# Gate projection of two token tiles as seven Strassen block products, with its weights prepared during the first feed-forward half

## What is computed

```python
D_MODEL = 1024; SEQ = 2048; D_FF = 2816; PLE_DIM = 256
...
hn = rmsnorm(h, g_ffn_norm[i])
h = h + (jax.nn.silu(hn @ w_gate[i]) * (hn @ w_up[i])) @ w_down[i]
gate = jax.nn.sigmoid(rmsnorm(h, g_ple_norm[i]) @ w_ple_gate[i])
h = h + gate * (p[i] @ w_ple_proj[i])
```

## Time and profile before

| | |
|---|---|
| median of three runs | 2041.3 us |
| span of the profiled execution | 2043.8 us |
| TensorE busy | 2014.7 us (99%), 9565 matmuls |
| VectorE busy | 1365.8 us (67%) |
| ScalarE busy | 900.5 us (44%) |
| GpSimd busy | 409.9 us (20%) |
| granted TensorE clock, mean | 0.997 of full |
| down section of half 0, us from the span's start | about 977 to 1187 |
| gate-and-embedding sections of half 0 | 1187 to 1297.5 |
| gate-and-embedding sections of half 1 | 1928 to 2038 |

### The profile page before, as it was taken

How to read it: one execution, slowest core, us unless ns; L and a number is a source line. 1 busy time by engine, 2 the same in 40 slices (tenths; PEclk the granted TensorE clock), 3 DMA queues, 4 the chain that set the end, 5 groups by cost and what they waited for, 6 DMA issues and landing times.

```text
span 2043.8 us, 26178 instructions
## 1 busy us (share of the span) xinstructions
PE 2014.7 (99%) x9565; PEld 1667.4 (82%) x9565; DVE 1365.8 (67%) x1904; ACT 900.5 (44%) x1461; POOL 409.9 (20%) x534
## 2 busy tenths in 40 slices
PE   8999999999999999999999999999999999999998
PEld 7887877877788888888888888888888888888887
DVE  4686664767686665665888765966566566987763
ACT  4585743757433333333333553533333333334542
POOL 5554644645420000000000220000000000001220
PEclk9999999999999999999999999999999999999999
DMA  8667556563933223224815029432322328342143
GB/s 194 196 186 249 192 187 219 176 237 128 347 133 122 89 70 96 83 73 165 313 57 170 21 78 237 139 119 68 95 87 69 99 80 290 138 148 81 50 134 103
DMA packets 195488, 292.10 MB, mean 143 GB/s; under 512 B 14661, under 2 KB 116429, under 8 KB 194080
## 3 DMA queue, kind: packets, MB, share of 16 engines
q1 hardware_dynamic: 172672, 212.97, 34.3%
q0 software_dynamic: 22544, 77.46, 11.2%
q10 hardware_dynamic: 144, 0.00, 0.0%
HBM read 223.25 MB, written 67.51 MB: 142 GB/s over the span
## 4 chain that ended last, share of the span: by engine, by line
PE 86%; DVE 5%; DMA 3%; issue 2%; ACT 2%; POOL 1%; SPq 0%; ACTq 0%; DVEq 0%; POOLq 0%
PE bank L2646 13%; PE bank L2648 13%; PE bank L2650 13%; PE bank L2685 7%; PE bank L2683 7%; PE bank L2684 7%; PE bank L2345 5%; PE bank L2347 5%; PE bank L2346 5%; PE bank L2321 2%; PE bank L2323 2%; PE bank L2322 2%; PE bank L2414 1%; DMA w_parts<-w_split 1%; PE bank L2427 1%
## 5 line engine op out<-in xcount | busy, mean ns | idle before, releaser
L2646 PE MATMUL bank<-a_hi,ring_hi 128*128 128x512 f32 x1232 | 480.4, 390 | 1.1 <-DVE ring_lo L1940 0.7
L2650 PE MATMUL bank<-a_hi,ring_lo 128*128 128x512 f32 x1232 | 479.9, 390 | 0.0
L2648 PE MATMUL bank<-a_lo,ring_hi 128*128 128x512 f32 x1232 | 479.9, 390 | 0.0
L2646 PEld LDWEIGHTS bank<-a_hi,ring_hi 128*128 128x128 f32 x1232 | 231.3, 188 | 50.1 <-DVE ring_lo L1940 1.4
L2650 PEld LDWEIGHTS bank<-a_hi,ring_lo 128*128 128x128 f32 x1232 | 231.3, 188 | 48.1
L2648 PEld LDWEIGHTS bank<-a_lo,ring_hi 128*128 128x128 f32 x1232 | 231.4, 188 | 47.5
L2683 PE MATMUL bank<-d_hi 128*128 128x512 f32 x616 | 240.1, 390 | 0.0
L2684 PE MATMUL bank<-d_lo,d_hi 128*128 128x512 f32 x616 | 240.0, 390 | 0.0
L2685 PE MATMUL bank<-d_hi,d_lo 128*128 128x512 f32 x616 | 239.9, 389 | 0.0
L1419 ACT ACTIVATE d_hi<-keep 128x1024 fp32r<-128x1024 f32 x132 | 139.8, 1061 | 201.9 <-PE bank L2685 184.9
L999 POOL DMA_DIRECT2D hidden_T<-hid x88 | 47.6, 541 | 770.5 <-DVE hid L1976 751.2
(11 more groups left out here) (271 smaller groups left out, 3889.9 us busy)
## 6 DMA issues: line engine op xcount, KB each, us to landing
w_parts<-w_split POOLq DMA_DIRECT2D x88, 512.0 KB, 4.6
hidden_T<-hid POOLq DMA_DIRECT2D x88, 256.0 KB, 2.3
raws<-in_w_gate SPq DMA_DIRECT2D x80, 256.0 KB, 4.7
raws<-in_w_up SPq DMA_DIRECT2D x80, 256.0 KB, 5.2
keep<-hidden_T SPq DMA_DIRECT2D x66, 256.0 KB, 3.8
raw<-in_w_ple_gate SPq DMA_DIRECT2D x64, 256.0 KB, 4.2
keep<-in_w_down SPq DMA_DIRECT2D x44, 256.0 KB, 4.1
other<-hidden_T SPq DMA_DIRECT2D x44, 256.0 KB, 6.8
```

The costliest lines, as they stand in the source:

```text
L2646: mm(dst[:, :], wh[:, g, cols], a_hi[o][:, k, :], start=fresh and k == 0, stop=False, skip_group_check=True)
L2648: mm(dst[:, :], wh[:, g, cols], a_lo[o][:, k, :], start=False, stop=False, skip_group_check=True)
L2650: ins = mm(dst[:, :], wl[:, g, cols], a_hi[o][:, k, :], start=False, stop=k == 3, skip_group_check=True)
```

## The change

`w_ple_gate` is treated as 2x2 blocks of 512x512 and the pair of tiles as a 2x2 block matrix (tile, feature half). The gate projection of the pair is then seven block products (`G_ONE`, `G_TWO`, `G_SIX`, `G_FIVE`, `G_SEVEN`, `G_THREE`, `G_FOUR`) of 48 matmuls each, in place of 2 tiles x 8 panels x 24 matmuls.

- The seven weight blocks (four of them sums) are made once, in the feed-forward section of half 0, in column blocks c = 2 to 9: GpSimd's queue loads four 128x512 pieces (`gate_blocks`), GpSimd forms four sums (`gate_block_sums`), and then, in seven items, ScalarE makes the hi into the single buffer `gw_hi` (`gate_block_hi`), GpSimd subtracts for the lo and stores hi and lo to DRAM (`gate_block_low`). ScalarE's next item waits until both stores of the one before have landed. Three items stand in an even block (after beats 2, 3, 4), four in an odd one (after beats 1, 2, 3, 4); two blocks make one of four sets.
- In `ple_section` the prepared panels come back by DMA (14 loads of 2 x 512 KB per half, three slots); `split` of gate panels is gone.
- VectorE makes eight sums of operand pieces per half (`operand_sum`), and `operand_hi`/`operand_lo` split 14 operand pieces.
- Four groups of four output pieces: products are added to copies of earlier ones (`copy_gate` on ScalarE, `add_products` on VectorE); for 12 of 16 pieces the last add goes to GpSimd (`add_gated`).
- TensorE's order: both projections of tile 0, `G_ONE` with the second tile's statistics inside it, both projections of tile 1, then the other six products.
- In half 0, only `a0`, `a2`, `a1` are split before the next feed-forward section; the rest of `a3` moves into its first beat, and ScalarE does the hi of `a3`, `a4`, `a5` there. `a1`'s hi waits for GpSimd's twelfth add (`ple_out` 12).
- Buffers move; waits follow them.

```diff
@@ constants
+G_ONE, G_TWO, G_SIX, G_FIVE, G_SEVEN, G_THREE, G_FOUR = range(PRODUCTS)
+G_BLOCKS = ((0, 0), (1, 1), (0, 1), (1, 0))
+G_PREP_FROM = 2
+G_ITEM_AT = ((2, 3, 4), (1, 2, 3, 4))
-A_ORDER = (0, 1, 3, 4, 2, 5, 6)
+A_ORDER = ((0, 1, 3, 4, 2, 5, 6), (0, 2, 1, 3, 4, 5, 6))
...
@@ gpsimd
+            def add_gated(half, n):
+                tile, e = G_BLOCKS[n // 4 % 4]
+                pool.wait_ge(ple_mul, n + 1)
+                v = h2[tile][:, 4 * e + n % 4, :]
+                nc.gpsimd.tensor_tensor(v, gate_buffer(n), v, ALU.add).then_inc(ple_out, 1)
...
+            def gate_block_low(k, i):
+                at = gate_block_of(i)
+                pool.wait_ge(wp_hi_done, 1 + PRODUCTS * k + i + 1)
+                nc.gpsimd.tensor_tensor(gw_lo[at][:, :], gw[at][:, :], gw_hi[:, :].bitcast(F32),
+                                        ALU.subtract).then_inc(wp_lo_done, 1)
...
+                pool.dma_start(g_split[n, 0][:, cols], gw_hi[:, :].bitcast(F32)).then_inc(band_stored, 16)
+                pool.wait_ge(wp_lo_done, 1 + (PRODUCTS + 4) * k + 4 + i + 1)
+                pool.dma_start(g_split[n, 1][:, cols], gw_lo[at][:, :].bitcast(F32)).then_inc(band_stored, 16)
...
                 for c in range(FPAIRS):
-                    if c:
-                        store_hid(half, c - 1, 3)
-                    for j in range(3):
-                        store_hid(half, c, j)
+                    for o in range(OPS):
+                        if o == 0 and c:
+                            store_hid(half, c - 1, 3)
+                        if half == 0 and o < 2:
+                            gate_weights(c, o)
+                        if o in (2, 5, 6):
+                            store_hid(half, c, (2, 5, 6).index(o))
+                        if half == 0 and o >= 2:
+                            gate_weights(c, o)
@@ scalar
+                if half:
+                    if o == 0:
+                        act.wait_ge(pp, 16)
+                    elif o in (1, 3, 4):
+                        act.wait_ge(ple_out, {1: 12, 3: 8, 4: 12}[o])
...
                         ffn_beat(half, c, o)
+                        if half and c == 0 and o < 3:
+                            a_part_hi(1, 3 + o)
+                        if half == 0:
+                            gate_weights(c, o)
...
+            def gate_block_hi(k, i):
+                at = gate_block_of(i)
+                done = PRODUCTS * k + i
+                act.wait_ge(consts, CONSTS + 64 * (k + 1))
+                if i >= 2:
+                    act.wait_ge(wp_lo_done, 1 + (PRODUCTS + 4) * k + 4)
+                if done:
+                    act.wait_ge(*gate_stored(done))
+                nc.scalar.activation(gw_hi[:, :], gw[at][:, :], ACT.Copy).then_inc(wp_hi_done, 1)
@@ vector
-                    if half == 0:
-                        a_rest(0, 3)
+                    a_rest(half, 3)
...
+                for first in (4, 8):
...
+                if half == 0:
+                    ring_part_lo(1, 0)
+                    a_rest(1, 1)
+                for b in range(12, 16):
+                    gated_rows(half, b)
@@ tensor
+            def ple_section(half):
+                gb = 2 * half + 1
                 for e in range(2):
...
+                    proj_block(half, 0, e)
+                gate_product(half, G_ONE, 0)
+                pe.wait_ge(pp_copied, copied_count(half, (0, 0), 0))
+                turn_squares(NORM3[gb], acc3, bank[BS1[0]])
+                gate_product(half, G_ONE, 1)
+                pe.wait_ge(pp_copied, copied_count(half, (0, 0), 3))
+                turn_rstd(NORM3[gb], bank[BS1[3]])
                 for e in range(2):
...
+                    proj_block(half, 1, e)
+                for r in range(2):
+                    gate_product(half, G_TWO, r)
+                for i in (G_SIX, G_FIVE, G_SEVEN, G_THREE, G_FOUR):
+                    for r in range(2):
+                        gate_product(half, i, r)
```

More of the change, by code:

```diff
@@ L943, in z_section, with gate_weights @@
+            def gate_weights(c, o):
+                k, second = divmod(c - G_PREP_FROM, 2)
+                if not 0 <= k < 4:
+                    return
+                if o == 0 and not second:
+                    gate_blocks(k)
+                if o == 1 and not second:
+                    gate_block_sums(k)
+                if o in G_ITEM_AT[second]:
+                    gate_block_low(k, G_ITEM_AT[second].index(o) + 3 * second)
             def z_section(t):
@@ new lines, in copy_gate @@
+            def copy_gate(half, i, b):
+                act.wait_ge(gt, gate_count(half, i, b))
+                if i == G_ONE:
+                    n = 16 * half + b
+                elif i == G_SIX:
+                    n = 16 * half + 8 + b
+                    act.wait_ge(pp, 16 * (half + 1))
+                else:
+                    n = 16 * half + 4 + b
+                    act.wait_ge(pT_lo, 2 * half + 2)
+                    act.wait_ge(acc_done, 7 * NORM3[2 * half + 1] + 7)
+                nc.scalar.activation(gate_buffer(n), bank[(BS0, BS1)[i % 2][b]][:, :], ACT.Copy).then_inc(pp_copied, 1)
```

713 lines of the change are left out of this document (443 added, 270 removed).

## The result

The changed kernel takes 2045.5 us, the median of 12 runs, beside 2041.1 for the kernel before in the same rounds: ratio 1.0020, 95% interval 1.0012 to 1.0028. It is slower by 0.2%; the forecast was 13 us faster. The profiled execution of the changed kernel has a span of 2042.0 us (that execution took 2043.8), so the two profiles are compared stage by stage, each from the first matmul of one stage to the first of the next. (The attention part ahead of them, which the change leaves alone, differs from execution to execution: the feed-forward begins at 556.4 us in the profile of before, at 550.6 in that of after, and between 549.4 and 555.4 in those of the experiments; the two of these that leave the kernel before's attention part as it is, e6 and e7, have 550.4 and 549.4.)

What follows compares the result with a forecast made beforehand. The prediction took TensorE, busy 99% of the span, as the bound: -21.8 + 5.6 + 0.6 + 0.5 + 2.0 = -13.1 us, from the profiled 2043.8 to 2030.7, less 2.5 for the median: 2028.2 us. Range 2019.5 to 2038.

Steps and rivals of the forecast that it cites:

- The matmuls removed, -21.8: Gate sections of both halves: 96 fewer matmuls at 0.2266 us each save 21.8 us.
- +0.6: Gate sections: the bank of `G_ONE` is free about 0.3 us late in each half, 0.6 us lost.
- The walk through block c = 4, +5.6: Feed-forward half 0: weight preparation delays ScalarE's second `u3` copy, TensorE losing 1.4 us in each of four even blocks.
- x: Landing time of the second item's last store in an even feed-forward block, taken as 3.6 us, bounds 2.3 and 4.8.
- From half 0 to half 1, +0.5 and +2.0: Half change: 0.5 us for GpSimd's longer adds beside VectorE, 2.0 us for `a3`'s extra lo in the first block.
- `ple_out` reaches 12 at E - 4.2: Half change: GpSimd's four adds and four stores of the last pieces it adds finish 4.2 us before E.
- E: The last gate matmul of half 0, from which the times of the half change are counted.
- The +2.0 for `a3`: First block of half 1: VectorE's additional 2048-column lo shifts work by 2.2 us with 0.2 to spare, losing 2.0 us.
- The end, 0: End of the kernel: the last four pieces are handled as before, so no time is gained or lost.
- C: Rival, feed-forward: preparation costs more than the products save, ScalarE waiting for DRAM stores at `gw_hi`; 2049.8 us, chance 0.18.
- D: Rival: GpSimd and VectorE hold each other up, adds taking 2.32 us at half change and end; 2035.6 us, chance 0.14.

Runs made afterwards that it cites:

- e6: Kernel before plus 13 spare 128x128 ScalarE copies ahead of the second `u3` bank's copy at blocks 2, 4, 6, 8 of feed-forward half 0; 2052.2 us.
- e7: Kernel before plus 9 spare 128x128 ScalarE copies ahead of the second `u3` bank's copy at each of blocks 2 to 9; 2051.3 us.
- e9: Changed kernel, but of gate panels 6 to 13 in half 0 only the first quarter of the columns is loaded; 2044.9 us.
- e12: e8 with VectorE's additions and multiplications for pieces 4 to 11 of half 0's gate over only 64 of 512 columns; 2029.6 us.
- e15: e12 with GpSimd's stores of pieces 4 to 11 issued behind all eight of its sums; 2025.0 us.
- e16: e8 with ring slot 1 first, pieces 4 to 7 before the third operand sum, two last pieces before `a1`, stores behind sums; 2027.0 us.
- e17: e8 with only GpSimd's stores of pieces 4 to 11 in half 0's gate moved behind their sums; 2029.2 us.
- e1: Changed kernel with a second place for the hi part, so ScalarE waits only for the stores of the item before last; 2036.4 us.
- e2: Changed kernel without any preparation of the gate's weight blocks; the gate reads other stored panels of the same size; 2029.7 us.
- e5: Changed kernel without GpSimd's four sums of a set of weight blocks, single hi buffer kept; 2031.5 us.
- e8: e1 with the second and third item of each set one beat later (operations 2, 4, 5 of the even block); 2029.5 us.

## Why the prediction was wrong, step by step

- **The matmuls removed, -21.8.** Right. The two gate stages are 19.6 us shorter, and the start of `G_ONE` takes most of the difference: 0.91 and 0.94 of waiting on a projection copy, 1.9 us where +0.6 was put down. The mechanism there was right, the size three times too small: ScalarE's last square ended 10.9 us into the section where 9.6 was put down, behind four sums of GpSimd that took 7.76 us together and not 4 x 1.33.
- **The walk through block c = 4, +5.6.** The mechanism is as forecast, ScalarE in front of `gw_hi`, then the `u` copy, and even x was: 3.37 us (736.22 to 739.59) where 3.6 was taken. What failed first is "Four sums of 1.33 us with hand-offs end at 728.9" and "the first lo ends at 730.8". In the time of the trace of before they ended at 729.9 and 732.2, since two sums and the lo took 1.70 to 1.75 beside VectorE, and the second store went out 0.4 later than put down. ScalarE's first stand ended 1.4 us later than forecast (735.5 for 734.1), the third item began 1.0 later (741.3 for 740.3). Listed waits: 3.6 (two at c = 2, where the loads took 5.6 us from the last issue to the first sum, for 3.4 at c = 4), 1.8, 2.2, 0.6 (c = 7, an odd block, where none was forecast), 1.9 and 0.2, in all 10.2. On top come what e6 and e7 measured: 0.3 for each of seven restarts, 2.1, and two half-clock stretches, 3.2. Together 15.5 of the 15.7. The prediction had neither term: "any new wait of TensorE is time lost, one for one" was wrong by half again.
- **From half 0 to half 1, +0.5 and +2.0.** The step that failed is "`ple_out` reaches 12 at E - 4.2". With E = 1297.5 it came at 1298.8, E + 1.3, 5.5 us late; from there the chain ran as written (forecast end E + 6.5, measured 1309.6, E + 12.1), and 5.6 us of lateness are the wait: 6.2 against 0.7. Behind it comes the half-clock stretch of 2.3; 5.5 and 2.3 are the 7.8 of this stage. The multiplications of these four pieces, put at E - 12.2 to E - 8.7, ran from E - 7.4 to E - 2.1. The walk began at them and never asked what stood before them on VectorE. There stood the operand sums, for a load issued at 1257.98 that landed 9.2 us later; the prediction dealt with those four loads only as a danger to the panels. In e9 VectorE began on that load 2.5 us earlier and the slot came 2.5 earlier, one for one; e12 and e15 show GpSimd's sums with their stores as the next bound right behind VectorE. The +2.0 for `a3` did not appear in the changed kernel; where the first wait is small, in e15, a wait of 0.8 us on that sum of VectorE shows.
- **The end, 0.** Right: last matmul to the end of the span 6.1 before, 6.2 after.
- **The rivals.** C (the preparation costs more than the products save) has the sign and nearly the size of what was lost, but not for its reason, a store landing at x over 5.4; x was 3.4. D named the mutual slowing, priced it at the half change and at the end, and refused it because "most of the 72 adds, many of them beside VectorE work, are near 1.33". At the half change it hardly came: the sums of pieces 8 to 11 took 1.28 to 1.43 us, only one of pieces 4 to 7 took 2.42, and the lateness was the load's. A median over the whole program says nothing on the few that run beside VectorE operations on two SBUF tiles, and in the feed-forward those are the ones that count. 2035.6 was given for D; its place in the feed-forward, where it ate the slack, was not priced.

The Trainium skill, page "SBUF — State Buffer", section "Who interferes with whom", says that a VectorE operation with two inputs in SBUF contends with GpSimd's reads and that one with at most one such input, outside the two-port modes, does not. The rows of the changed kernel agree with both parts of it: while GpSimd's sum of 1290.85 runs, the addition from a PSUM bank takes 0.68 us as elsewhere, and the multiplication of two SBUF tiles behind it 1.40 instead of 0.68. By that rule the prediction's sum would have used the slower durations wherever such operations meet.

What stays open: in e16 TensorE still loses about 5 us at the half change, 2.8 of it on the first bank copy of half 1. No order tried removed it. Which share of the half change's loss is due to the load, to VectorE's queue and to GpSimd's is not split further than e9, e12, e15 and e17 do, since each relief makes another of them the last.

## What to carry to other kernels

When work is added to an engine that also frees banks at fixed times, write the added chain with its slowest durations and see what stands behind it in that engine's queue: here a second buffer and one constant (a beat later) gave back 16 us that the same work had cost. Price a wait of TensorE at its listed length plus 0.3 us, and for one of about 2 us or more add a possible half-clock stretch (1.6 us and more here). Walk every chain back to a load or to TensorE itself, through each engine's queue, before trusting a time counted from its middle, and use the slower durations for work moved from VectorE to GpSimd where both work on SBUF operands at once.

## What was unexpected of the hardware

- Each TensorE wait cost 0.3 us more than listed: eight of 0.90 us made a stage 9.8 us longer (e7).
- Half clock (1.2 GHz, matmuls 0.427 us apart) followed one of four equal waits of 2.27 us (e6), two of the changed kernel's five waits of 1.75 to 2.16 in its first feed-forward, and none of eight of 0.9 us (e7); it followed every wait of 6 us seen here (changed, e1, e2, e5, e8, e17).
- A 128x512 sum on GpSimd took 1.28 to 2.42 us and a 128x1024 lo on VectorE 1.22 to 2.31 us, the long ones in rows where the other engine worked on SBUF tiles at the same time.
